# Ordering a long convolution's frequency-domain stages by two channel halves

## The chip, the cores and the metric

The kernel runs on one core of one Trainium2 chip. The metric is the device time of one execution in microseconds; smaller is better. Before the change three runs took 2891.93, 2896.40 and 2896.47 us (median 2896.4).

## The reference, cut to what matters

The program is one large block (a gated linear recurrence and a long convolution, then a mixture of 16 experts) followed by a block of two further layers. The change is inside the long convolution, for 256 positions and 1024 channels, run twice in a row (n = 0 and 1):

```python
filt = hyena_filters(S, filt_w1, filt_b1, filt_w2, filt_b2, filt_w3, filt_freq)   # taps, times a decay
z = v.astype(f32)
for n, gate in enumerate((x1, x2)):
    k = bidir_kernel(filt[:, n, 0], filt[:, n, 1])
    z = gate.astype(f32) * fftconv(z, k, filt_bias[n])     # irfft(rfft(z) * rfft(k)) + z * bias
y_b = z.astype(dt) @ w_b_out
```

Every channel is convolved by itself, so channels 0 to 511 need nothing of channels 512 to 1023 in any of these steps.

## The kernel before, in words

Five engines run programs of their own and wait for one another through semaphores. TensorE multiplies, VectorE does the two-operand arithmetic, ScalarE copies and computes functions, POOL and SP issue transfers. TensorE executes its program strictly in the written order.

The transform is done by matmuls with fixed matrices: `fwd` (two row tiles of 128 positions by 512 columns, real parts then imaginary parts of 256 frequencies) and `inv` (four row tiles by 256 positions). All data are float32. A matmul here writes 128 rows by 512 channels, one bank of `psx`. For each n the stages are, in the order of the code:

- taps (L705 to L710): 8 groups of one matmul with 64 rows of contraction, for two position tiles `tt`, two channel halves `half` and two directions `d`. VectorE (L1729 to L1744) multiplies each by the decay (into `f0` and `f1`), clears a row and adds the bias if `tt` is 0, and writes the sum and the difference into `taps_s` and `taps_d`. Below, the work for one pair of `tt` and `half` is called a quarter. When all four quarters are done it raises `taps_ready`.
- spec_k (L713 to L720): TensorE waits for `taps_ready` and transforms the taps, 8 groups of two matmuls (four row tiles `m`, two halves). ScalarE copies each group to `spec_k` in SBUF (L1294 to L1297).
- spec_u (L723 to L732): TensorE transforms the signal `v_tok`, 8 groups of two matmuls (halves, two frequency tiles `f`, real and imaginary). For n = 1 it waits for `z_tok` first. VectorE (L1745 to L1760) multiplies each by `spec_k`, reading the bank four times for one pair, and raises `spec_y` for each of the four pairs.
- inverse (L733 to L746): TensorE waits for all four steps of `spec_y`, and computes 4 groups, of 4 matmuls each for n = 0 (L739) and of 8 half-wide ones for n = 1 (L744). VectorE multiplies each by x1 (n = 0, back into `v_tok`, then `z_tok`) or by `x2` (n = 1).

The order around the change is set by a plan of banks, `small_plan()`: a list of all groups in the order in which TensorE makes them, with the engine that reads each. Four banks rotate; before a group is made, `claim` waits until the group four places earlier in the list has been read:

```python
        if g >= 4 and self.reader[g - 4]:
            pe.wait_ge(self.sems[self.reader[g - 4]], self.count[g - 4])
        return self.banks[g % 4]
```

So the order in the plan, that on TensorE and those on the readers must be the same. `was_read` waits until a group has been read, and `x_ready` until it has been made.

Behind the convolution `x2` is split into a high and a low part by ScalarE and VectorE (`cut_acts`, with the semaphore `z_cut`), and TensorE multiplies by `w_b_out` and `w_o` (L554). The weights of these products pass a ring of four buffers (SP, L2222). The experts' weights pass 16 buffers (SP, L2240); the first 16 transfers wait for `z_cut`, `merged` and the ring's last buffers, every later one for the matmuls (L813, L841) that used its buffer. POOL loads the filter's weights (the second set once the last tap group of n = 0 is made) and, behind `z_tok`, the router's weights and `memT`.

Of the kernel before, what the change touches and what calls it, by code (L numbers as in the profile page):

```python
# [25 lines left out]
TT = T // P  # L26
# [189 lines left out]
def small_plan():  # L216

    plan = []

    def add(reader, *key):  # L220
        plan.append((key, reader))

    add("act", "norm", "g_mix")
    for part in ("v", "x1"):
        for i in range(4):
            add("act", "hy_tr", part, i)
    for d in range(2):
        for kind in range(2):
            for i in range(4):
                add("act", "lru", d, kind, i)  # L230
    add("dve", "filt", 0)
    add("dve", "filt", 1)
    for n in range(2):
        for tt in range(TT):
            for half in range(2):
                for d in range(2):
                    add("dve", "taps", n, tt, half, d)
        for m in range(4):
            for half in range(2):
                add("act", "spec_k", n, m, half)  # L240
        for half in range(2):
            for f in range(2):
                for im in range(2):
                    add("dve", "spec_u", n, half, f, im)
        for i in range(4):
            add("dve", "inv", n, i)
    add("act", "norm", "g_ffn")
    add("act", "norm_mem")
    add("dve", "router")
    for tt in range(TT):  # L250
        for i in range(2):
            add("act", "h_tok", tt, i)
    for i in range(4):
        add("dve", "moe_acc", i)
    add("act", "norm", "g_final")
    for l in range(LAYERS):
        add("act", "norm", f"norm_ffn1{l}")
        for i in range(4):
            add("dve", "ffn1", l, i)
        add("act", "norm", f"norm_mix{l}")  # L260

        for i in range(3):
            add("act", "qk_norm", l, i)
        add("act", "av_tr", l, 0)
        add("act", "av_tr", l, 1)
        for h in range(6):
            for it in range(2):
                add("dve", "score", l, h, it)
        for h in range(6):
            add("act", "prob_tr", l, h)  # L270
        for q in range(HP):
            add("act", "att", l, q)
        add("act", "pool", l)

        for i in range(2):
            add("act", "kk_norm", l, i)
        for kind in range(3):
            for i in range(2):
                add("act", "lora", l, kind, i)
        if l:  # L280
            add("act", "vdown", l)
            for i in range(2):
                add("act", "vup", l, i)
        for tt in range(TT):
            for x in "abkv":
                add("dve" if x == "b" else "act", "rw_tr", l, tt, x)
            for x, r in (("A", "dve"), ("AT", "dve"), ("BT", "dve"), ("CT", "dve"), ("DT", "dve"),
                         ("P2", "act"), ("P2T", "act"), ("Q2", "dve"), ("P4", "act"), ("P4T", "act"), ("Q4", "dve"),
                         ("P8", "act"), ("Q8", "dve"), ("TR", "act"), ("X1", "act"), ("Q32", "dve"),
                         ("BV", "act"), ("WU", "act")):  # L290
                for p in range(2):
                    add(r, x, l, tt, p)
            for q in range(HP):
                add("dve", "M", l, tt, q)
                add("dve", "N", l, tt, q)
                add("dve", "RY", l, tt, q)
            for c in range(4):
                add("dve", "S", l, tt, c)
            for p in range(2):
                add("dve", "y", l, tt, p)  # L300
        for x, r in (("mean", "dve"), ("var", "act"), ("bonus", "dve")):
            for i in range(2):
                add(r, x, l, i)
        add("act", "norm", f"norm_cross{l}")
        add("act", "xnorm", l, "q", 0)
        for h in range(4):
            for it in range(2):
                add("dve", "xscore", l, h, it)
        for h in range(4):
            add("act", "xprob_tr", l, h)  # L310
        for h in range(4):
            add("dve", "xatt", l, h)
        add("act", "norm", f"norm_ffn2{l}")
        for i in range(4):
            add("dve", "ffn2", l, i)
    return plan


def program(nc, A, out):
    ctx = ExitStack()  # L320
    with ctx:
# [11 lines left out]
        def S(name):  # L333
            if name not in sems:
                sems[name] = ctx.enter_context(nc.semaphore(name))
            return sems[name]
# [197 lines left out]
        def _(pe):  # L534
# [167 lines left out]
            pe.wait_ge(S("dft_in"), 16)  # L702
            for n in range(2):
                pe.wait_ge(S(f"w3_in{n}"), 16)
                for tt in range(TT):  # L705
                    for half in range(2):
                        for d in range(2):
                            b = XB.claim(pe, ("taps", n, tt, half, d))
                            done(pe.matmul(b[:, :], sq[0:64, 2, tt * P:(tt + 1) * P], w3h[:, d, half, :],
                                           start=True, stop=True))  # L710

                pe.wait_ge(S("taps_ready"), n + 1)
                for m in range(4):  # L713
                    src = taps_s if m < 2 else taps_d
                    for half in range(2):
                        b = XB.claim(pe, ("spec_k", n, m, half))
                        for tt in range(TT):
                            mm = pe.matmul(b[:, :], fwd[:, tt, m * P:(m + 1) * P],  # L718
                                           src[:, tt, half * 512:(half + 1) * 512], start=(tt == 0), stop=(tt == 1))
                        done(mm)  # L720
                if n:
                    pe.wait_ge(S("z_tok"), 4)
                for half in range(2):  # L723
                    for f in range(2):
                        for im in range(2):
                            b = XB.claim(pe, ("spec_u", n, half, f, im))
                            m = 2 * im + f
                            for tt in range(TT):
                                mm = pe.matmul(b[:, :], fwd[:, tt, m * P:(m + 1) * P],
                                               v_tok[:, tt, half * 512:(half + 1) * 512],  # L730
                                               start=(tt == 0), stop=(tt == 1))
                            done(mm)  # L732
                pe.wait_ge(S("spec_y"), 4 * (n + 1))  # L733
                for i in range(4):
                    b = XB.claim(pe, ("inv", n, i))
                    if n == 0:
                        tt, half = i // 2, i % 2
                        for m in range(4):
                            mm = pe.matmul(b[:, :], inv[:, m, tt * P:(tt + 1) * P],  # L739
                                           spec_y[:, m, half * 512:(half + 1) * 512], start=(m == 0), stop=(m == 3))  # L740
# [392 lines left out]
        def _(act):  # L1133
# [157 lines left out]
                act.drain()  # L1291
            act.drain().then_inc(S("decay"), 1)
            for n in range(2):
                for m in range(4):  # L1294
                    for half in range(2):
                        b = x_ready(act, "spec_k", n, m, half)
                        read(copy(spec_k[:, m, half * 512:(half + 1) * 512], b[:, :]))  # L1297
            cut_acts(x2, h_hi)
            for i in range(4):
# [177 lines left out]
        def _(dve):  # L1477
# [248 lines left out]
            f0, f1 = (sq[:, i:i + 2, :].rearrange("p a t -> p (a t)") for i in (4, 6))  # L1726
            dve.wait_ge(S("bias_in"), 16)
            for n in range(2):
                for tt in range(TT):  # L1729
                    for half in range(2):  # L1730
                        cs = slice(half * 512, (half + 1) * 512)
                        for d, dst in ((0, f0), (1, f1)):
                            b = x_ready(dve, "taps", n, tt, half, d)
                            read(tt_(dst, b[:, :], decay[:, tt, cs], ALU.mult))
                        dve.drain()
                        if tt == 0:
# [4 lines left out]
                        tt_(taps_s[:, tt, cs], f0, f1, ALU.add)  # L1741
                        tt_(taps_d[:, tt, cs], f0, f1, ALU.subtract)
                        dve.drain()
                dve.drain().then_inc(S("taps_ready"), 1)  # L1744
                XB.was_read(dve, ("spec_k", n, 3, 1))  # L1745
                for half in range(2):
                    cs = slice(half * 512, (half + 1) * 512)
                    for f in range(2):
                        kr, ki = spec_k[:, f, cs], spec_k[:, 2 + f, cs]
# [11 lines left out]
                for i in range(4):  # L1761
                    b = x_ready(dve, "inv", n, i)
                    if n == 0:
                        tt, cs = i // 2, slice((i % 2) * 512, (i % 2 + 1) * 512)
                        read(tt_(v_tok[:, tt, cs], b[:, :], x1_tok[:, tt, cs], ALU.mult))
                    else:
                        read(tt_(x2[:, 2 * i:2 * i + 2, :], m2(b), x2[:, 2 * i:2 * i + 2, :], ALU.mult))
                if n == 0:
                    dve.drain().then_inc(S("z_tok"), 4)
            cut_acts(x2, "z_cut")  # L1770
            for i in range(4):
                cut_ahead(cutter, ("w_b_out", i))
# [606 lines left out]
```

## Time and profile before

| what | us |
|---|---|
| median of three runs | 2896.4 |
| profiled execution | 2899.57 |
| its span in the trace | 2897.4 |
| TensorE matmul busy | 2442.4 (84%) |
| VectorE busy | 1206.7 (42%) |
| ScalarE busy | 844.5 (29%) |

The profiled execution is one run with the recorder on; times inside it count from the start of the span. A row of the timeline gives the start, the duration, the engine, the line of the code, the operation with its output and inputs, how many such in a row, and in brackets how long the engine had been idle and what released it. One float32 matmul of the code leaves two MATMUL records. Tiles that are parts of one large tensor carry its name: `scr` and `hx` stand for nearly all the tiles of the convolution (`taps_s`, `taps_d` and `spec_y` lie in `hx`, `spec_k`, `v_tok`, `x1_tok`, `x2`, `fwd` and `inv` in `scr`), and `f0` and `f1` lie in `sq`. VectorE's two-operand operations all have the line of a helper, L1485, and ScalarE's copies L1138. The convolution runs from about 254 to 391 us.

### The profile page before, as it was taken

To read this page: it belongs to the slowest core of one execution; us is meant where nothing else is said; L and a number is where in the kernel's file an instruction comes from. 1 tells how busy PE (TensorE), PEld (TensorE's weight loads), DVE (VectorE), ACT (ScalarE), POOL (GpSimd) and SP (SyncE) were. 2 spreads that over 40 slices of the span, in tenths; PEclk is the share of its full clock that TensorE was granted. 3 is DMA by queue.
4 is the path that set the end of the run, shared out by engine and by line. 5 is a ranking of instruction groups with operands and counts; after the bars stand their busy time and mean duration, and the time that the engine had idled before them with its cause. 6 is when DMAs were issued, how large, how long until landed. Compare 5 with 4: busy or idle time off the path is not lost.

```text
span 2897.4 us, 43617 instructions
## 1 busy us (share of the span) xinstructions
PE 2442.4 (84%) x18480; PEld 1906.1 (66%) x18480; DVE 1206.7 (42%) x1767; ACT 844.5 (29%) x1204; POOL 115.5 (4%) x109
## 2 busy tenths in 40 slices
PE   6898888877777777777789997799999998779999
PEld 6896376332233332223289985689999997668999
DVE  6756453100000000000065667556556566656655
ACT  3383021100000000000044444244445444324543
POOL 0000012000000000000010010000001001000000
PEclk9998888988888888888899996789999998679999
DMA  6434036999999999999945540034555554003453
GB/s 219 152 124 153 16 132 262 425 425 425 425 424 425 425 424 425 426 425 425 426 172 187 177 168 1 30 117 141 180 189 193 179 175 139 2 30 117 162 188 117
DMA packets 118619, 669.79 MB, mean 231 GB/s; under 512 B 10683, under 2 KB 12902, under 8 KB 60993
## 3 DMA queue, kind: packets, MB, share of 16 engines
q1 hardware_dynamic: 113376, 650.14, 57.4%
q0 software_dynamic: 2784, 13.21, 1.3%
q10 hardware_dynamic: 2304, 4.20, 0.4%
q8 instruction: 120, 1.97, 0.3%
q14 instruction: 35, 0.28, 0.0%
HBM read 662.26 MB, written 5.24 MB: 230 GB/s over the span
## 4 chain that ended last, share of the span: by engine, by line
PE 52%; DMA 20%; DVE 10%; SPq 7%; ACT 3%; issue 3%; DVEq 3%; POOLq 1%; POOL 0%; ACTq 0%; PEldq 0%; PEld 0%
PE psd L554 27%; PE psx L554 8%; DMA ring<-in_w_up 7%; SPq L2240 7%; DMA ring<-in_w_down 4%; DMA hx<-in_w_down 2%; DMA ring<-in_w_gate 2%; PE psd L813 2%; DVE w_lo L1485 2%; DMA hx<-in_w_up 2%; PE psd L804 1%; PE psx L986 1%; PE psx L855 1%; PE psd L841 1%; DVE scr L1485 1%
## 5 line engine op out<-in xcount | busy, mean ns | idle before, releaser
L554 PE MATMUL psd<-h_hi,w_hi 128*128 128x256 f32 x2448 | 703.4, 287 | 51.1 <-DVEq L1515 24.9
L1485 DVE TENSOR_TENSOR w_lo<-ring,w_hi 128x1024 fp32r<-128x1024 f32 x436 | 523.4, 1242 | 450.4 <-ACT w_hi L1145 447.7
L554 PE MATMUL psd<-h_lo,w_hi 128*128 128x256 f32 x2448 | 698.0, 285 | 0.0
L554 PE MATMUL psd<-h_hi,w_lo 128*128 128x256 f32 x2448 | 697.7, 285 | 0.0
L1145 ACT ACTIVATE w_hi<-ring 128x1024 fp32r<-128x1024 f32 x436 | 435.2, 1046 | 329.6 <-PE psd L554 324.6
L554 PEld LDWEIGHTS psd<-h_hi,w_hi 128*128 128x128 f32 x2448 | 475.6, 194 | 57.1 <-DVEq L1515 26.4
L554 PEld LDWEIGHTS psd<-h_lo,w_hi 128*128 128x128 f32 x2448 | 475.7, 194 | 0.3
L554 PEld LDWEIGHTS psd<-h_hi,w_lo 128*128 128x128 f32 x2448 | 475.3, 194 | 0.0
L554 PE MATMUL psx<-halves,w_hi 128*128 128x256 f32 x1408 | 255.6, 283 | 3.2 <-issue 3.2
L554 PEld LDWEIGHTS psx<-halves,w_hi 128*128 128x128 f32 x1408 | 219.6, 192 | 3.9 <-issue 3.9
L1485 DVE TENSOR_TENSOR scr<-psd,scr 128x512 f32<-128x512 f32 x20 | 13.8, 690 | 497.8 <-PE psd L813 497.8
L554 PE MATMUL psx<-halves,w_lo 128*128 128x256 f32 x704 | 199.2, 283 | 0.0
L1138 ACT ACTIVATE scr<-psd 128x512 f32<-128x512 f32 x48 | 28.6, 596 | 579.1 <-PE psd L819 357.1
L813 PE MATMUL psd<-scr 128*32 128x512 f32 x768 | 135.0, 824 | 63.3 <-DMA scr<-in_w_up 58.1
L813 PE MATMUL psd<-ring,scr 128*32 128x512 f32 x512 | 88.2, 787 | 56.6 <-DMA ring<-in_w_up 41.5
L554 PEld LDWEIGHTS psx<-halves,w_lo 128*128 128x128 f32 x704 | 135.1, 192 | 0.0
L1842 DVE COPY scr<-psd 128x512 f32<-128x512 f32 x16 | 11.1, 692 | 294.9 <-PE psd L841 294.9
L813 PEld LDWEIGHTS psd<-scr 128*32 128x32 f32 x768 | 22.5, 129 | 164.6 <-DMA scr<-in_w_up 127.2
L554 PE MATMUL psd<-halves,w_hi 128*128 128x256 f32 x640 | 119.2, 289 | 3.0 <-DVE halves L1485 3.0
L1138 ACT ACTIVATE scr<-psx 128x192 f32<-128x192 f32 (+4 forms) x125 | 53.9, 439 | 191.9 <-PE psx L718 87.5
L554 PEld LDWEIGHTS psd<-halves,w_hi 128*128 128x128 f32 x640 | 102.4, 196 | 3.5 <-DVE halves L1485 3.2
L813 PEld LDWEIGHTS psd<-ring,scr 128*32 128x32 f32 x512 | 12.8, 121 | 121.3 <-DMA ring<-in_w_up 85.0
(344 smaller groups left out, 2942.9 us busy)
## 6 DMA issues: line engine op xcount, KB each, us to landing
ring<-in_ffn_wi SPq DMA_DIRECT2D x88, 1024.0 KB, 4.8
scr<-in_w_gate SPq DMA_DIRECT2D x48, 1024.0 KB, 19.9
scr<-in_w_down SPq DMA_DIRECT2D x48, 1024.0 KB, 22.4
scr<-in_w_up SPq DMA_DIRECT2D x48, 1024.0 KB, 27.0
ring<-in_ffn_wo SPq DMA_DIRECT2D x44, 1024.0 KB, 4.9
ring<-in_w_gate SPq DMA_DIRECT2D x32, 1024.0 KB, 19.0
ring<-in_w_up SPq DMA_DIRECT2D x32, 1024.0 KB, 26.7
ring<-in_w_down SPq DMA_DIRECT2D x32, 1024.0 KB, 22.9
```

The lines of the kernel that those rows point to most:

```text
L554: mm = pe.matmul(o, w[u], a[v], start=start and i == 0, stop=stop and i == 2, **kw)
L804: mm = pe.matmul(psd[0][:, k * CAP:(k + 1) * CAP], h_tok[:, tt, k * P:(k + 1) * P], onehot[:, tt, bass.ds(2 * pair + e, 1), :].rearrange(" ...
L813: mm = pe.matmul(psd[t // 8][32 * j:32 * j + 32, :], xs[:, t % 8, :], e_ring[s % ERING][:, j * 512:(j + 1) * 512], start=(t % 8 == 0), sto ...
L841: mm = pe.matmul(psd[2 + half][32 * j:32 * j + 32, :], actT[:, kt_ % 4, 32 * (kt_ // 4):32 * (kt_ // 4) + 32], down_rows(n)[:, j % 2, half ...
L855: pe.matmul(acc[k // 2][:, k % 2, :], ye[:, k // 4, (k % 4) * P:(k % 4 + 1) * P], PT, start=False, stop=False, skip_group_check=True)
L986: mm = pe.matmul(tri(b, n)[r, q, :], MATS[lhs][p][r, q, :], rhs(p, q)[r, :], start=True, stop=True)
L1138: return act.activation(o, i, ACT.Copy)
L1145: act.activation(w_hi[j % 2][:, c], ring[n % RING][:, c], ACT.Copy).then_inc(hi_cut, 1)
L1485: return dve.tensor_tensor(o, a, b, op)
L1842: dve.tensor_copy(ye[:, 1, :], psd[3][:, :]).then_inc(S("ye_ready"), 1)
L2240: sp.dma_start(dst, src).then_inc(e_land[s % ERING], 16)
```

## The change

Each loop over channel halves moves outside the loop over the position tiles `tt` or the row tiles `m`, in the plan and on the three engines alike. `taps_ready` is raised once for each half, and TensorE waits for it once for each half, ahead of that half's four spec_k groups. The inverse waits for two steps of `spec_y` ahead of its first two groups and for all four ahead of the last two; for n = 0 its groups are ordered so that the first two are the first half. For n = 1 they are unchanged, as group i covers channels 256 i to 256 i + 255. `z_tok` is raised in two steps of 2. No matmul and no arithmetic operation is added or taken away.

```diff
@@ small_plan
-        for tt in range(TT):
-            for half in range(2):
+        for half in range(2):
+            for tt in range(TT):
                 for d in range(2):
-                    add("dve", "taps", n, tt, half, d)
-        for m in range(4):
-            for half in range(2):
-                add("act", "spec_k", n, m, half)
+                    add("dve", "taps", n, half, tt, d)
+        for half in range(2):
+            for m in range(4):
+                add("act", "spec_k", n, half, m)
@@ TensorE
-                for tt in range(TT):
-                    for half in range(2):
+                for half in range(2):
+                    for tt in range(TT):
                         for d in range(2):
-                            b = XB.claim(pe, ("taps", n, tt, half, d))
+                            b = XB.claim(pe, ("taps", n, half, tt, d))
...
-                pe.wait_ge(S("taps_ready"), n + 1)
-                for m in range(4):
-                    src = taps_s if m < 2 else taps_d
-                    for half in range(2):
-                        b = XB.claim(pe, ("spec_k", n, m, half))
+                for half in range(2):
+                    pe.wait_ge(S("taps_ready"), 2 * n + half + 1)
+                    for m in range(4):
+                        src = taps_s if m < 2 else taps_d
+                        b = XB.claim(pe, ("spec_k", n, half, m))
...
-                if n:
-                    pe.wait_ge(S("z_tok"), 4)
                 for half in range(2):
+                    if n:
+                        pe.wait_ge(S("z_tok"), 2 * half + 2)
...
-                pe.wait_ge(S("spec_y"), 4 * (n + 1))
                 for i in range(4):
+                    if i % 2 == 0:
+                        pe.wait_ge(S("spec_y"), 4 * n + i + 2)
                     b = XB.claim(pe, ("inv", n, i))
                     if n == 0:
-                        tt, half = i // 2, i % 2
+                        tt, half = i % 2, i // 2
@@ ScalarE
-                for m in range(4):
-                    for half in range(2):
-                        b = x_ready(act, "spec_k", n, m, half)
+                for half in range(2):
+                    for m in range(4):
+                        b = x_ready(act, "spec_k", n, half, m)
@@ VectorE
-                for tt in range(TT):
-                    for half in range(2):
-                        cs = slice(half * 512, (half + 1) * 512)
+                for half in range(2):
+                    cs = slice(half * 512, (half + 1) * 512)
+                    for tt in range(TT):
...
-                dve.drain().then_inc(S("taps_ready"), 1)
-                XB.was_read(dve, ("spec_k", n, 3, 1))
+                    dve.drain().then_inc(S("taps_ready"), 1)
                 for half in range(2):
+                    XB.was_read(dve, ("spec_k", n, half, 3))
...
                     if n == 0:
-                        tt, cs = i // 2, slice((i % 2) * 512, (i % 2 + 1) * 512)
+                        tt, cs = i % 2, slice((i // 2) * 512, (i // 2 + 1) * 512)
...
-                if n == 0:
-                    dve.drain().then_inc(S("z_tok"), 4)
+                    if n == 0 and i % 2:
+                        dve.drain().then_inc(S("z_tok"), 2)
```

## Rows read from the trace of the kernel before

**Rows 1.** The page, part 4: shares of the chain that ended last, by engine.

```profile
PE 52%; DMA 20%; DVE 10%; SPq 7%; ACT 3%; issue 3%; DVEq 3%; POOLq 1%; POOL 0%; ACTq 0%; PEldq 0%; PEld 0%
```

**Rows 2.** Busy us by stretch: PE, PEld, DVE, ACT, POOL; granted clock, DMA share, GB/s.

```profile
254.00:395.00 141.00, 111.89 (x258) 53.12 (x258) 66.53 (x104) 17.63 (x26) 2.36 (x3) 0.85 0.07 23
...
460.00:510.00 50.00, 43.98 (x260) 27.95 (x263) 11.84 (x32) 6.46 (x13) 19.07 (x17) 0.79 0.57 230
510.00:1480.00 970.00, 715.90 (x4373) 314.31 (x4366) 82.12 (x142) 84.68 (x121) 5.60 (x3) 0.84 0.99 415
```

**Rows 3.** The timeline of TensorE in the convolution: start, duration, operation, count, idle before.

```profile
261.14 3.78 PE L709 MATMUL psx<-scr,sq 64*128 64x512 f32 x4 [2.66 <-DVE sq L1485]
265.12 3.78 PE L709 MATMUL psx<-scr,sq 64*128 64x512 f32 x4 [0.20 <-DVE sq L1485]
273.91 17.04 PE L718 MATMUL psx<-hx,scr 128*128 128x512 f32 x32 [5.01 <-DVEq L1744]
290.78 13.90 PE L729 MATMUL psx<-scr 128*128 128x512 f32 x32
309.14 16.49 PE L739 MATMUL psx<-hx,scr 128*128 128x512 f32 x32 [4.46 <-DVEq L1760]
325.56 5.41 PE L709 MATMUL psx<-scr,sq 64*128 64x512 f32 x12
331.72 1.98 PE L709 MATMUL psx<-scr,sq 64*128 64x512 f32 x4 [0.74 <-DVE sq L1485]
...
340.51 16.17 PE L718 MATMUL psx<-hx,scr 128*128 128x512 f32 x32 [6.81 <-DVEq L1744]
356.51 13.90 PE L729 MATMUL psx<-scr 128*128 128x512 f32 x32
374.88 15.77 PE L744 MATMUL psx<-scr,hx 128*128 128x256 f32 x64 [4.47 <-DVEq L1760]
```

**Rows 4.** The timeline of VectorE in the convolution.

```profile
264.37 1.29 DVE L1485 TENSOR_TENSOR sq<-psx,scr 128x512 f32<-128x512 f32 x2
...
268.35 1.29 DVE L1485 TENSOR_TENSOR sq<-psx,scr 128x512 f32<-128x512 f32 x2
...
271.10 1.29 DVE L1485 TENSOR_TENSOR sq<-psx,scr 128x512 f32<-128x512 f32 x2
...
292.77 1.29 DVE L1485 TENSOR_TENSOR hx<-psx,scr 128x512 f32<-128x512 f32 x2 [18.99 <-PE psx L729]
...
301.20 1.29 DVE L1485 TENSOR_TENSOR hx<-psx,scr 128x512 f32<-128x512 f32 x2
...
325.67 0.69 DVE L1485 TENSOR_TENSOR scr<-psx,scr 128x512 f32<-128x512 f32 x1 [2.74 <-PE psx L739]
...
330.97 1.29 DVE L1485 TENSOR_TENSOR sq<-psx,scr 128x512 f32<-128x512 f32 x2
```

**Rows 5.** Single microseconds by engine; the third value from the right is the granted clock.

```profile
266.00:267.00 1.00, 1.00 (x3) 0.34 (x2) 0.93 (x3) 0.00 (x0) 0.00 (x0) 0.50 0.00 0
...
281.00:282.00 1.00, 1.00 (x4) 0.48 (x3) 0.00 (x0) 0.28 (x1) 0.00 (x0) 1.00 0.00 0
...
334.00:335.00 1.00, 0.00 (x0) 0.00 (x0) 0.93 (x3) 0.00 (x0) 0.00 (x0) 0.83 0.00 0
```

**Rows 6.** The timeline of ScalarE: two of its copies of spec_k, n = 0.

```profile
282.40 0.60 ACT L1138 ACTIVATE scr<-psx 128x512 f32<-128x512 f32 x1 [1.12 <-PE psx L718]
284.12 0.60 ACT L1138 ACTIVATE scr<-psx 128x512 f32<-128x512 f32 x1 [1.12 <-PE psx L718]
```

**Rows 7.** The chain in order of time: where w_b_out starts.

```profile
394.70 25.42 PE psd L554 x192
```

**Rows 8.** The timeline of SP's transfers behind the convolution.

```profile
412.54 15.19 SPq L2240 DMA_DIRECT2D scr<-in_w_gate  x6
...
452.02 0.48 SPq L2258 DMA_DIRECT2D scr<-in_x_wkv  x1
484.91 6.51 SPq L2240 DMA_DIRECT2D scr<-in_w_down  x6
```

More of the change, by code:

```diff
@@ L1728, in _ @@
             for n in range(2):
-                for tt in range(TT):
-                    for half in range(2):
-                        cs = slice(half * 512, (half + 1) * 512)
+                for half in range(2):
+                    cs = slice(half * 512, (half + 1) * 512)
+                    for tt in range(TT):
                         for d, dst in ((0, f0), (1, f1)):
-                            b = x_ready(dve, "taps", n, tt, half, d)
+                            b = x_ready(dve, "taps", n, half, tt, d)
                             read(tt_(dst, b[:, :], decay[:, tt, cs], ALU.mult))
```

## The prediction

> **What bounds the kernel now.** First the shares of the chain of waits [rows 1]: TensorE holds about half of it, the transfers a fifth. A share over the whole span says nothing of one stage, so next the busy times by stage [rows 2]. From 510 to 1480 us the DMA engines are 0.99 busy: that is the experts' stream. The stretch that the change touches is 254 to 395 us: DMA share 0.07, ScalarE busy for 17.6 us of 141, TensorE for 111.9, VectorE for 66.5. No transfer and no third engine can set its time; it is TensorE and VectorE taking turns. Then the timeline of TensorE in it [rows 3], where the reader is to look at the idle time in brackets. It stops four times for VectorE: 5.01 us ahead of the taps' transform (L718, n = 0), 4.46 us ahead of the inverse (L739), 6.81 us ahead of L718 again (n = 1) and 4.47 us ahead of L744. The transforms of the signal (L729) have no wait ahead of them. The other side is VectorE [rows 4]: it idles for 18.99 us ahead of 292.77, while TensorE transforms the taps, and between the inverse's groups. Each stop costs twice. The granted clock [rows 5] is 1.00 in dense work, which is the 2.4 GHz level, and 0.50, which is 1.2 GHz, after a stop. ScalarE's copies [rows 6] give the price of one 512-column group of two matmuls: 1.72 us at the upper level (284.12 - 282.40). VectorE's reads of the inverse give 3.43 us for a group of four (2.74 of waiting and 0.69 of reading, at 325.67) [rows 4]. Eight groups of two, or four of four, are 13.8 and 13.7 us. The rows of the transforms are longer: 16.87 us (290.78 - 273.91), 16.42 (325.56 - 309.14), 16.00 (356.51 - 340.51) and 15.77 [rows 3]. So the lower level costs 3.1, 2.7, 2.3 and 2.0 us behind the four stops.
>
> **The change, part by part.** It removes no matmul and no vector operation. It reorders them by channel half and puts a semaphore step behind each half. The only added instructions are two more drains of VectorE for the taps and one for the product with x1.
>
> Part 1, taps to their transform, n = 0. VectorE works a quarter of the taps in 3.98 us where the row tile is 0 (268.35 - 264.37, with a memset and the bias) and 2.75 us where it is 1 (271.10 - 268.35) [rows 4]. The new order is 0, 1, 0, 1 in place of 0, 0, 1, 1, so the first half is ready 2.75 us behind 264.37, at 267.1 us. TensorE's last tap matmuls wait for the read at 264.37, which the new order has at the same time, so they start at 265.12 and end at 268.9 as now [rows 3]. The banks are claimed in written order, so the transform's first group also needs the read of the fifth tap group, at 267.1 + 0.7 = 267.8, and groups two to four need the reads at 268.5, 271.8 and 272.4. None is late. The transform starts at 268.9 instead of 273.91 and the second half's flag (273.9) is up before its first group. The whole idle time, 5.0 us, goes. The start is at the lower level: the clock is 0.50 through the taps, though TensorE is fully busy in them [rows 5]. The four starts before paid 2.0 to 3.1 us; I take 2.6, where this one paid 3.1: 0.5 more. Part 1 gives 5.5 us; bounds 5.0 and 8.1 (nothing paid for the clock).
>
> Part 2, product to inverse, n = 0. VectorE works the second half from 301.20 [rows 4] until L739 can start at 309.14 [rows 3], 4.0 us for a frequency tile, and is slower than TensorE here. So the first half's product is done at 301.1 and all of it at 309.1, both in the time of the old trace. Now inverse groups 1 and 2 need the first half alone, and the banks of spec_u's last four groups. The first of these are read by 302.5 (301.20 + 1.29) and by 303.8, one more pair of operations later, and TensorE ends L729 at 290.78 + 13.90 = 304.7 [rows 3]. So group 1 starts at 304.7, group 3 at 311.5, when the second half has been ready for 2.4 us. The stop of 4.46 us goes, and with it the 2.7 us of clock, as TensorE never halts: 7.2 us. Bounds 4.5 (the clock is lower all the same) and 7.2. VectorE's reads are behind its own product, which ends at 309.1, in both orders; four banks hold four groups, so nobody is held up.
>
> Part 3, taps to transform, n = 1. In the time of the old trace VectorE begins the second quarter at 330.97 [rows 4]; it is now a short one of 2.75, so the first half is up at 333.8. Then the bank order binds: group 1 needs a read that ends at 334.5, groups 3 and 4 the reads at 338.5 and 339.2. TensorE ends the taps at 333.7 [rows 3], starts at 334.5, does two groups to 337.9, waits 0.6 us, does two more to 341.9 and the second half's four to 348.8; the flag for that half is up at 340.6. Before it was 356.51. That is 7.7 us at the upper level. But the row of 334 to 335 us shows the clock falling within 1.3 us of the taps' end [rows 5]. If it falls here as well and two groups go at half speed, the 0.6 us wait hides a part, and the end is 350.4 to 351.1. I take 349.6, between: 6.9 us, bounds 5.4 and 7.7.
>
> Part 4, product to inverse, n = 1. As part 2: columns of groups 1 and 2 (L744) lie in the first half. 4.47 us of stop and 2.0 us of clock: 6.5 us, bounds 4.5 and 6.5. The split wait for z_tok comes to nothing: in VectorE's order all four products with x1 stand ahead of the taps of n = 1, and these ahead of all that TensorE does behind that wait.
>
> Added: three drains. A short quarter is two pairs of operations of 1.29 us and two drains, 2.75 in all, so a drain costs 0.08 us [rows 4]; only those of n = 1 lie on the path: -0.2 us, bounds 0 and -0.6. On SP and POOL nothing is moved; POOL waits for z_tok's last step and for the same last tap group as before, and its loads go out 13 us earlier, into idle DMA engines.
>
> The sum is 5.5 + 7.2 + 6.9 + 6.5 - 0.2 = 25.9 us. What follows moves along with it: cutting x2 and the first matmul of w_b_out at 394.70 [rows 7] hang on the last read; that stage starts at the lower level in the old trace and I leave it so (bound: 2.3 us more if it doesn't). The experts' first transfers [rows 8] go out at 412.54, released step by step by this chain; the last of the first sixteen has left by 452.02, and the next one leaves at 484.91, when the first expert's matmuls free a buffer. DMA share in 460 to 510 us is 0.57 [rows 2], so the stream is started by the compute chain and shifts as a whole.
>
> The profiled execution took 2899.6 us (span 2897.4 and 2.2 around it), 3.2 above the median of the runs, 2896.4. 2899.6 - 25.9 = 2873.7; on the median's footing 2870.5. All ends low: 5.0 + 4.5 + 5.4 + 4.5 - 0.6 = 18.8, so 2877.6; all high: 8.1 + 7.2 + 7.7 + 6.5 + 2.3 = 31.8, so 2864.6. The runs of before differ by 4.5 us among themselves, which widens both ends by 2 to 3 us.
>
> **The rivals.** (A) The bank rotation takes back the early start: if TensorE in truth gets no bank until the second half's last taps are read, L718 starts at 272.4 and at 339.2, and parts 1 and 3 give 1.5 and 1.3 us. Against it: the reads above, each computed from rows. Gain 16.3, time 2880. Chance 0.05.
>
> (B) Given back later: the stream or the clock of the many stages behind takes the gain, 2896. For it: those stages are two thirds of the time, and the transfers hold a fifth of the chain [rows 1]. Against: the idle DMA engines ahead of 484.91. Chance 0.04.
>
> (C) Slower: the clock. The new order lets TensorE creep along behind VectorE's reads, and the clock stays at 0.50 in all of the convolution. For it: the taps at 261 to 269 us, which stay at 0.50 for 8 us of almost unbroken work [rows 3, 5]. Against: all four transforms reach 1.00, and L729 holds it beside a slower VectorE. Price: behind 268.9 us lie six transforms of 13.8 us and the taps of n = 1 with 6.9, 89.7 us at the upper level; all at the lower they end at 448 us instead of 390.65, and the time is 2954. It decides from 52 us at the lower level more than I count on, as each costs half. Chance 0.02. The Trainium skill (TensorE: Matmul & The Clock Gate, section on psum-queue depth-cycling) speaks for it: a loop that cycles through PSUM banks and idles TensorE for short moments between groups was seen to swing between the two levels. So far the trace agrees for the taps only.
>
> **How the numbers follow.** The forecast has 0.89, A 0.05, B 0.04, C 0.02. A measurement of this kernel tells 0.2%, 5.8 us, from no change. Faster: the forecast, A, 0.94. Same: B, 0.04. Slower: C, 0.02. The range, 2862 to 2881, is the sum's bounds and the runs' spread; it takes in A.
>
> **What would show it.** In the trace after: L718 (n = 0) starts within 0.5 us of the taps' end; no idle time ahead of L739 and L744; L718 (n = 1) has two short waits of under 1 us in place of 6.81; the first w_b_out matmul stands near 369 us; granted clock 1.00 from about 274 us to the end of L739; the first refill of a buffer near 459 us. It would be wrong if L739 still waited for both halves, if the clock fell between the groups of L718, or if the first expert's matmuls didn't move by the same 26 us.

## The result and the profile after

The changed kernel took 2870.3 us (median of 4 runs, 2868.58 to 2870.71) against 2896.4 (2891.93 to 2899.29): a ratio of 0.991, 95% interval 0.9893 to 0.9927, or 26 us with 21 to 31 inside the interval. The forecast was 2870.5. The profiled execution took 2870.71 us, its span is 2868.6.

First the timeline of TensorE in the convolution of the changed kernel, to be held against [rows 3]. L718 is the taps' transform, L740 and L745 are the two inverses (L739 and L744 before).

```profile
256.69 3.70 PE L709 MATMUL psx<-scr,sq 64*128 64x512 f32 x8 [0.71 <-ACT sq L1287]
263.05 3.78 PE L709 MATMUL psx<-scr,sq 64*128 64x512 f32 x4 [2.66 <-DVE sq L1486]
267.03 3.78 PE L709 MATMUL psx<-scr,sq 64*128 64x512 f32 x4 [0.20 <-DVE sq L1486]
270.74 16.17 PE L718 MATMUL psx<-hx,scr 128*128 128x512 f32 x32
286.75 13.90 PE L729 MATMUL psx<-scr 128*128 128x512 f32 x32
300.48 13.90 PE L740 MATMUL psx<-hx,scr 128*128 128x512 f32 x32
314.31 5.41 PE L709 MATMUL psx<-scr,sq 64*128 64x512 f32 x12
320.46 1.98 PE L709 MATMUL psx<-scr,sq 64*128 64x512 f32 x4 [0.74 <-DVE sq L1486]
323.40 15.43 PE L718 MATMUL psx<-hx,scr 128*128 128x512 f32 x32 [0.95 <-DVE sq L1486]
338.67 13.90 PE L729 MATMUL psx<-scr 128*128 128x512 f32 x32
352.40 13.98 PE L745 MATMUL psx<-scr,hx 128*128 128x256 f32 x64
```

The brackets of 5.01, 4.46 and 4.47 us are gone. That of 6.81 has become 0.95, and its releaser is no longer the flag (DVEq) but a product of VectorE into `sq`, that is the read of the fifth tap group's bank. Both inverses last 13.9 to 14.0 us where they lasted 16.5 and 15.8: they run at the upper level of the clock from their first matmul.

The granted clock stands third from the right in the busy times by stretch, as in [rows 5]. It is 1.00 from 275 us to the end of the second taps, and three pieces at 0.50 are left: to 275 us, from 323 to 326 and from 371 to 374. The row of the single microsecond 322 to 323 shows that the second of these began in the idle time between the taps and L718, not among the groups of L718.

```profile
270.00:275.00 5.00, 5.00 (x6) 1.85 (x6) 4.54 (x8) 0.45 (x1) 0.51 (x1) 0.50 0.41 105
275.00:323.00 48.00, 46.70 (x108) 19.93 (x106) 25.48 (x41) 4.33 (x8) 1.85 (x2) 1.00 0.08 24
322.00:323.00 1.00, 0.45 (x2) 0.00 (x0) 0.83 (x2) 0.00 (x0) 0.00 (x0) 0.96 0.00 0
323.00:326.00 3.00, 2.60 (x3) 1.18 (x4) 2.71 (x6) 0.00 (x0) 0.00 (x0) 0.50 0.00 0
326.00:370.00 44.00, 40.38 (x126) 23.69 (x124) 23.18 (x37) 6.97 (x12) 0.00 (x0) 1.00 0.00 0
371.00:374.00 3.00, 3.00 (x16) 3.00 (x15) 0.00 (x0) 0.00 (x0) 0.00 (x0) 0.50 0.00 0
```

What follows the convolution has moved with it: the chain's first w_b_out matmul [rows 7], and SP's transfers [rows 8].

```profile
366.41 0.69 DVE scr L1486
...
370.43 24.80 PE psd L554 x192
```

```profile
387.65 15.18 SPq L2241 DMA_DIRECT2D scr<-in_w_gate  x6
...
426.95 0.44 SPq L2259 DMA_DIRECT2D scr<-in_x_wkv  x1
459.81 6.36 SPq L2241 DMA_DIRECT2D scr<-in_w_down  x6
```

To compare stages, times are counted from the first tap matmul, 254.78 us before and 256.69 after (the stage ahead of it is the same code and took 1.9 us longer in this execution).

| stretch (us) | before | after | difference |
|---|---|---|---|
| first tap matmul to first w_b_out matmul | 139.92 | 113.74 | -26.2 |
| to the first refill of an expert buffer | 90.21 | 89.38 | -0.8 |
| to the first matmul of the layers | 983.52 | 981.99 | -1.5 |
| to the end of the span | 1428.97 | 1426.80 | -2.2 |

The four differences add up to 30.7 us, and less the 1.9 us of the stage ahead they make the 28.8 us between the two spans. Only the first row is the change's. The second row varies by 2.1 us (88.07 to 90.21) among the five profiled kernels whose code behind the first w_b_out matmul is the same; 0.6 of its 0.8 us is w_b_out itself, whose row lasts 24.80 us where it lasted 25.42. The third row lies between 982.0 and 983.5 us in seven of the eight kernels profiled here (986.7 in one), the last between 1424.6 and 1429.3 us, all with the same code there, so the differences of 1.5 and 2.2 us are no effect of the change. The experts' stream took none of the gain back.

### The profile page after: what moved, and what is told of

Its sections match the earlier page's. It is cut to its first block, busy times and chain, and to the rows that moved or that the text cites. A ratio compares the mean times of both kernels' runs of the same rounds, so it can differ in the third digit from the quotient of the medians.

```text
span 2868.6 us, 43627 instructions
## 1 busy us (share of the span) xinstructions
PE 2435.4 (85%) x18480; PEld 1903.3 (66%) x18480; DVE 1206.8 (42%) x1767; ACT 844.5 (29%) x1204; POOL 115.4 (4%) x109
## 4 chain that ended last, share of the span: by engine, by line
PE 53%; DMA 21%; DVE 9%; SPq 6%; ACT 3%; issue 3%; DVEq 3%; POOLq 1%; POOL 0%; ACTq 0%; PEldq 0%; PEld 0%
PE psd L554 28%; PE psx L554 8%; DMA ring<-in_w_up 7%; SPq L2241 6%; DMA ring<-in_w_down 4%; DMA hx<-in_w_up 3%; DMA ring<-in_w_gate 2%; PE psd L814 2%; DVE w_lo L1486 2%; DMA hx<-in_w_down 2%; DMA scr<-in_w_gate 2%; PE psd L805 1%; PE psx L987 1%; PE psx L856 1%; DVE scr L1486 1%
## 5 line engine op out<-in xcount | busy, mean ns | idle before, releaser
L1843 DVE COPY scr<-psd 128x512 f32<-128x512 f32 x16 | 11.1, 692 | 287.3 <-PE psd L842 287.3
```

The source lines that it names most:

```text
L1843: dve.tensor_copy(ye[:, 1, :], psd[3][:, :]).then_inc(S("ye_ready"), 1)
```

## The experiments

Each was run beside the kernel before, in 4 or 5 timed runs. The kernel before had medians of 2896.4, 2896.7 and 2896.6 us in the three sets of runs, so the kernels of different sets are compared by their times as they stand.

**The inverse alone.** The kernel before, with the second wait split and the inverse's groups of n = 0 ordered by halves (on TensorE and VectorE), and nothing else.

```diff
-                pe.wait_ge(S("spec_y"), 4 * (n + 1))
                 for i in range(4):
+                    if i % 2 == 0:
+                        pe.wait_ge(S("spec_y"), 4 * n + i + 2)
...
-                        tt, half = i // 2, i % 2
+                        tt, half = i % 2, i // 2
```

> The kernel before with parts 2 and 4 alone: taps, their transform and both flags as before, the inverse waits for two steps of spec_y and then for all four. Theory (the four stops give their price one by one): the stops of 4.46 and 4.47 us ahead of the inverse go, with 2.7 and 2.0 us of clock; gain 13.7 us, time 2882.7, and the stops of 5.0 and 6.8 us ahead of L718 stay. Rival (only the whole order pays, since the first half is available earlier only if its taps are): gain under 5 us.

It took 2881.98 us (2879.35 to 2884.89), ratio 0.9952 (0.9938 to 0.9965). From the first tap matmul to w_b_out it is 125.9 us, 14.0 under the kernel before. The timeline of TensorE:

```profile
275.18 16.69 PE L718 MATMUL psx<-hx,scr 128*128 128x512 f32 x32 [5.01 <-DVEq L1745]
291.71 13.90 PE L729 MATMUL psx<-scr 128*128 128x512 f32 x32
305.44 13.90 PE L740 MATMUL psx<-hx,scr 128*128 128x512 f32 x32
...
334.22 16.19 PE L718 MATMUL psx<-hx,scr 128*128 128x512 f32 x32 [6.81 <-DVEq L1745]
```

The stops ahead of L718 stand to the hundredth; that ahead of the inverse is gone. The inverse needs no reordered taps. The rival is out.

**The taps alone.** The changed kernel, with one wait for all four steps ahead of the inverse.

```diff
+                pe.wait_ge(S("spec_y"), 4 * (n + 1))
                 for i in range(4):
-                    if i % 2 == 0:
-                        pe.wait_ge(S("spec_y"), 4 * n + i + 2)
```

> The changed kernel, but the inverse waits for all four steps of spec_y as before. Theory: parts 1 and 3 alone, 5.9 and 6.6 us as the trace after has them; gain 12.5 us, time 2884; a stop of 4.4 to 4.5 us stands ahead of both inverses and the clock falls behind them. With the run before this one the gains add up to 26 us. Rival (the parts overlap, one hides the other): the two gains add up to clearly more or less than 26.

It took 2884.12 us (2881.31 to 2885.48), ratio 0.9955 (0.9941 to 0.9968); the stretch is 126.8 us, 13.1 less than before. TensorE's timeline has the inverses' stops back, and not those of the taps:

```profile
286.51 13.90 PE L729 MATMUL psx<-scr 128*128 128x512 f32 x32
304.94 15.70 PE L739 MATMUL psx<-hx,scr 128*128 128x512 f32 x32 [4.53 <-DVEq L1760]
...
329.66 15.58 PE L718 MATMUL psx<-hx,scr 128*128 128x512 f32 x32 [0.95 <-DVE sq L1485]
```

The two gains in the trace are 14.0 and 13.1, together 27.1 against 26.2 for the whole change. In the medians they are 14.7 and 12.6, together 27.2 against 26.2. The parts add to within 1 us. Most of that microsecond is the clock: the inverse of n = 0 takes 15.63 us from its start to the next taps here, behind a stop of 4.53 us, and took 16.42 behind one of 4.46 in the kernel before. So what the lower level cost behind a stop of nearly one length differed by 0.8 us between these two executions.

**Keeping the clock up.** The changed kernel with matmuls of no use where TensorE idles: for n = 0 three behind the first half's taps and two behind the next pair, for n = 1 one behind the last taps, and four ahead of w_b_out. Their results are not read.

```diff
+            def fill(count):
+                for _ in range(count):
+                    pe.matmul(psd[3][:, :], fwd[:, 0, 0:P], fwd[:, 1, :], start=True, stop=True)
...
+                        if n == 0 and half + tt:
+                            if (half, tt) == (0, 1):
+                                DB.was_read(pe, ("w_a_out", 3))
+                            fill((0, 3, 2, 0)[2 * half + tt])
+                        if n == 1 and half and tt:
+                            fill(1)
...
+            fill(4)
             pe.wait_ge(S("z_cut"), 1)
```

> The changed kernel with extra float32 matmuls of 128 rows into an unused bank where TensorE idles: 3 and 2 among the taps of n = 0, 1 behind the taps of n = 1, 4 ahead of w_b_out. Their results are never read. Theory (TensorE's idle time lowers the clock, and that costs 2.25 us in L718 n = 0, 1.5 in n = 1 and 2.0 in w_b_out): granted clock 1.00 through all of it, L718 13.8 us long in both, gain over the changed kernel 5 to 6 us, time 2864.5. Rival (the taps with 64 rows of contraction pull the clock down whatever stands between them): L718 n = 0 still starts at 0.50 and the gain is 2 to 3.5 us. Second rival (a filler delays the first matmul behind it by more than the clock gives): no gain or a loss of up to 2 us.

It took 2867.88 us (2863.9 to 2869.17), 2.4 under the changed kernel in the medians and short of the 5 to 6 expected. Its convolution is 111.3 us, 2.4 less, and the first refill comes 198.06 us after the first tap matmul instead of 203.12. Of these 5.1 us, 2.4 lie in the convolution and 1.5 in w_b_out (its row lasts 23.31 us instead of 24.80, from 368.31); the other 1.2 lie between w_b_out and the refill, where kernels with the same code differ by as much, so they can't be put down to the fillers. The stretches behind the refill, the same code, were 2.1 us longer in the profiled execution. The two medians differ by less than the runs of one kernel do (2863.9 to 2869.17), so the total can't show such a part, and the stretch can. By stretch, the clock:

```profile
256.00:270.00 14.00, 12.54 (x29) 4.55 (x27) 10.12 (x16) 5.89 (x6) 0.14 (x1) 1.00 0.31 119
270.00:284.00 14.00, 13.55 (x31) 5.92 (x32) 5.59 (x10) 4.18 (x7) 0.36 (x1) 1.00 0.17 37
320.00:321.00 1.00, 1.00 (x2) 0.47 (x2) 0.83 (x3) 0.00 (x0) 0.00 (x0) 0.61 0.00 0
```

For n = 0 the first theory holds: 1.00 from the first taps through L718, and the first rival is out there. For n = 1 it fails: the clock fell at about 320.2 us, as the filler began, behind 8 us of taps with 0.74 us of idle time among them, and the gain there was nil (24.46 us from the taps to the signal's transform against 24.36). The second rival holds there: with the filler ahead of it the taps' transform starts 9.90 us behind the taps instead of 9.09, and what it then saves (14.56 us long instead of 15.27) only makes up for that. The timeline of L718 (L729 in this kernel) for n = 0 shows one thing more:

```profile
270.24 3.67 PE L729 MATMUL psx<-hx,scr 128*128 128x512 f32 x8 [0.68 <-DVE sq L1498]
274.12 10.57 PE L729 MATMUL psx<-hx,scr 128*128 128x512 f32 x24 [0.22 <-DVE sq L1498]
```

At the upper level TensorE is quick enough to meet the bank rotation: 0.68 us ahead of the first group and 0.22 ahead of the third. This is the mechanism of rival A, at 0.9 us and not at the 9.6 of its price.

**Useful matmuls in the idle time.** Behind the change TensorE is what the convolution waits for, all but while VectorE works the taps. The signal's transform doesn't depend on the taps, so the first half's four groups are put among the tap matmuls, in the four dense banks.

```diff
+                def early(g):
+                    f, im = g // 2, g % 2
+                    m = 2 * im + f
+                    if n == 0:
+                        DB.was_read(pe, ("w_a_out", g))
+                    for tt in range(TT):
+                        mm = pe.matmul(psd[g][:, :], fwd[:, tt, m * P:(m + 1) * P], v_tok[:, tt, 0:512],
+                                       start=(tt == 0), stop=(tt == 1))
+                    mm.then_inc(S("u_early"), 1)
...
+                        if (half, tt) == (0, 1):
+                            if n:
+                                pe.wait_ge(S("z_tok"), 2)
+                            early(0)
+                            early(1)
+                        elif half:
+                            early(2 + tt)
```

> The changed kernel with the first half's four spec_u groups put among the taps matmuls, into the four dense banks that are free there: two behind the first half's taps, one behind each pair of the second half's. Theory (behind the change TensorE is the bound of the convolution from the taps on, and idles only while VectorE works the taps): 6.9 us of matmuls move into idle time for n = 0 and the clock stays up, 9 us; n = 1 gains its 1.7 us of idle and 1.5 of clock; in all 12 us, time 2858. Rival (VectorE is the bound as soon as the order is loose, since a half's product takes it 8.0 us against 6.9 of TensorE): gain under 5 us, with idle time ahead of the inverse again.

It took 2858.79 us (2858.41 to 2866.69), 11.5 under the changed kernel; ratio to the kernel before 0.9868 (0.9853 to 0.9883). The timeline of TensorE for n = 0, where L719 are the taps and L711 the moved groups:

```profile
260.06 3.70 PE L711 MATMUL psd<-scr 128*128 128x512 f32 x8
263.69 1.98 PE L719 MATMUL psx<-scr,sq 64*128 64x512 f32 x4
265.60 1.98 PE L711 MATMUL psd<-scr 128*128 128x512 f32 x4
267.51 1.98 PE L719 MATMUL psx<-scr,sq 64*128 64x512 f32 x4
269.42 1.98 PE L711 MATMUL psd<-scr 128*128 128x512 f32 x4
271.24 13.90 PE L735 MATMUL psx<-hx,scr 128*128 128x512 f32 x32
284.98 7.03 PE L746 MATMUL psx<-scr 128*128 128x512 f32 x16
291.84 13.90 PE L757 MATMUL psx<-hx,scr 128*128 128x512 f32 x32
```

No bracket is left in the convolution, for n = 1 neither, and the granted clock is 1.00 in all of it (256 to 355 us); the first one stands ahead of w_b_out, 4.05 us. The stretch to w_b_out is 102.7 us, 11.1 less than in the changed kernel: 8.4 for n = 0 and 2.7 for n = 1, where 9 and 3.2 had been expected. VectorE did not become the bound. The profiled execution was the one of 2866.69 us, 8 above the three others; its excess lies behind the convolution (986.7 us of expert stream against 982.0), so only the convolution is read from it.

**The next wait for all, split too.** x2 is split into high and low parts only when all four inverse groups are multiplied, because the parts go to where `spec_y` lies, which the inverse reads to its end. Here each quarter of x2 is cut at once, into a free place (72 to 88 KiB of the scratch); in exchange two of the experts' first transfers, which go there, wait for the last w_b_out product.

```diff
+        z_halves = sb("z_halves", [P, 2 * KD * T], F32R)
...
-            pe.wait_ge(S("z_cut"), 1)
             for i in range(4):
-                dense(("w_b_out", i))
+                dense(("w_b_out", i), (z_hi, z_lo), ready=None if i else ("z_cut", 0))
@@ VectorE
+                        dve.drain().then_inc(S("act_made"), 1)
+                        low(x2, z_hi, z_lo, i, "z_cut")
@@ SP
+                elif s == ERING_SCR + 3:
+                    sp.wait_ge(slots_done, SN[("w_b_out", 3)] + 1)
```

> The changed kernel, with the split of x2 joined in the same way: each quarter of x2 is cut as soon as its inverse group has been multiplied, into a place of its own, and the first w_b_out product waits for one quarter at a time. Two of the experts' first transfers wait for the last w_b_out product in exchange. Theory (a wait for all where a part would do costs its idle time and the clock behind it): the 4.05 us ahead of w_b_out and 1.8 us of clock in it go, 5.8 us, time 2864.5. Rival (the two transfers held back, or VectorE's added steps between the inverse's reads, take it back): under 2 us of gain.

It took 2864.69 us (2861.12 to 2865.56), 5.6 under the changed kernel; ratio 0.9886 (0.9869 to 0.9903). In the trace w_b_out starts 109.3 us behind the first tap matmul, 4.4 sooner, without a stop, and its row in the chain (192 matmuls) ends 132.7 us behind it instead of 138.5: 5.8 sooner, as expected.

```profile
364.31 23.05 PE psd L557 x192
```

```profile
379.78 15.19 SPq L2244 DMA_DIRECT2D scr<-in_w_gate  x6
```

The two transfers that were held back show no cost: SP's queue reached the first six only at 379.78 us, behind the last transfers of w_o, and they took 15.19 us as in the other kernels.

**Both.** The last two together, no further edit.

> The signal's first half among the taps, as in the run with spec_u in free banks, and the split by quarters together. Theory: gains on different stops add, 11.5 + 5.8 = 17.3 us under the changed kernel, time 2853; granted clock 1.00 from the taps of n = 0 into w_o. Rival (the stages behind give a part back, as the expert stream starts from a fixed release): under 12 us.

It took 2851.36 us (2845.92 to 2852.01), 18.9 under the changed kernel and 45 under the kernel before; ratio 0.9839 (0.9824 to 0.9854). The granted clock over the whole convolution and the start of w_b_out, and w_b_out in the chain:

```profile
254.00:343.00 89.00, 88.30 (x211) 38.65 (x210) 61.39 (x97) 15.45 (x22) 2.36 (x3) 1.00 0.13 38
343.00:363.00 20.00, 20.00 (x130) 18.73 (x129) 8.04 (x12) 4.53 (x6) 0.00 (x0) 1.00 0.00 1
```

```profile
353.62 23.05 PE psd L556 x192
```

TensorE is busy for 108.3 of 109 us at 1.00. In the trace w_b_out's row ends 121.7 us behind the first tap matmul, 16.9 sooner than in the changed kernel, and that is the 11.1 and the 5.8 of the two kernels before. In the medians the single gains of 11.5 and 5.6 make 17.1, and 18.9 were measured; the difference is inside the spread of the runs (2845.92 to 2852.01). So the gains add, as expected, and the rival is out. It is the fastest version here, and with TensorE busy throughout there is next to nothing left to win in this stretch by order alone.

## Why the prediction was right

The sum was 25.9 us, the stretch gave 26.2. By the sum's own steps, read as differences of the starts of L729, the second taps, L729 again and the last read, each from the first tap matmul:

| part | forecast | measured |
|---|---|---|
| 1, taps to transform, n = 0 | 5.5 | 5.9 |
| 2, product to inverse, n = 0 | 7.2 | 7.2 |
| 3, taps to transform, n = 1 | 6.9 | 6.6 |
| 4, product to inverse, n = 1 | 6.5 | 6.4 |
| drains | -0.2 | within the parts |

The mechanism was right in all four parts. That the sum came out to 0.3 us is in part luck: parts 1 and 3 missed by 0.4 and 0.3 in opposite directions, mostly through the two prices of the clock, and one such price differed by 0.8 us between two executions above. That the median came out to 0.2 us is more luck, as the runs of one kernel differ by 2 to 11 us among themselves.

Part 1. The whole 5.01 us of idle time went, as forecast. The start at the lower level cost 2.25 us (16.01 from 270.74 to 286.75, less 13.76 for eight groups of 1.72) where I took 2.6: the clock rose after 275 us. It fell in the 2.66 us of idle time ahead of the taps at 263.05 us (0.50 from 262 us) and stayed at 0.50 through them. The run with fillers, in which both stretches hold matmuls of 128 rows, stayed at 1.00; whether it is the filled idle time or the matmuls among the taps that kept it up, that run doesn't tell.

Part 2. Exact: L740 starts right behind L729 and the clock is 1.00 throughout. The inverse-alone run shows this part by itself: 27.56 us from L729 to the second taps, in both kernels, against 34.78 before.

Part 3. The bank order bound where I said, at the fifth tap group's read: 0.95 us of idle time against 0.8. The clock did fall (0.50 from 323 us), which I had weighed and taken at half price; the row costs 15.27 us from start to start, 1.5 above the upper level. My bound for that case was worked out too kindly: two groups of 3.44 us from 334.5, then six of 1.72 end at 351.7 and not at 351.1, so the part's lower bound should have been 4.8 and not 5.4. The measured end lies at 349.9 in the time of the old trace, so this didn't bear on the outcome. The short wait ahead of the third group that I forecast isn't there, since at the lower level the first two groups took long enough to hide it. One of my signs ("two short waits") was therefore wrong, and the range of this part held it.

Part 4. As part 2.

What stayed at its price: w_b_out still starts 4.02 us behind the start of the last read, and the clock is lower behind this stop too (0.50 from 371 to 374 us, and from 393 to 399 before), as I had left it. The stream was released by the compute chain and shifted as a whole: the refill stands at 459.81 against 459 forecast, and counted from the first tap matmul it came 27.0 us sooner (203.12 for 230.13).

The rivals. A, that the bank rotation takes the early start back: its mechanism exists, at 0.95 us in the changed kernel and 0.9 in the one with fillers, not at its price. B, that a later stage gives the gain back: the stream's length is the same within 1.5 us, and in the first two experiments, too. C, the clock at 0.50 through the whole convolution: not seen in any run. The section of the Trainium skill that spoke for it (TensorE: Matmul & The Clock Gate, on psum-queue depth-cycling) describes a swing of the level when TensorE idles briefly and often between groups as it cycles through banks. The traces show single such waits only: those of 0.68 and 0.22 us ahead of and inside L718 left the clock at 1.00 in the kernel with fillers, while it fell during the one of 0.95 us behind the second taps in the changed kernel. Whether frequent ones would do what the page says, no run here shows.

## What to carry to other kernels

When two engines take turns on data whose parts are independent, look at the brackets ahead of each stage: in the kernel before each of the four stops cost its idle time and then 3 to 6 us at the lower level of the clock, and both can be read from its rows. Split such a wait only down to the first part that is ready early, check each claim of a rotating buffer against the reads behind it, and then fill what idle time is left with work that doesn't depend on it; here that was worth 11.5 us, where the change gave 26. Read small parts by stretch from a common event, as the total of this kernel wanders by 5 us.

## What the runs showed of the hardware

TensorE's idle time alone doesn't tell where the clock was up. In the changed kernel the taps, matmuls with 64 rows of contraction, ran from 263 to 270.8 us with 0.20 us of idle time between them, at 0.50 throughout; the level rose 4.3 us into L718, whose matmuls have 128 rows. With fillers the clock fell at 320.2 us behind 8 us of such taps, with under 1 us of idle time among them. In the two kernels with spec_u groups of 128 rows between the same taps it stayed at 1.00 through the convolution. That it is the rows that count, and not the short idle times between, was not tried by itself.

Nor did a stop of one length always lower the clock. In the products behind the convolution TensorE stops for 3.01 us in the changed kernel (ahead of 402.53 us) and in the last one (ahead of 383.98). In the changed kernel the granted clock was 0.50 from 402 to 408 us; in the last one it was 1.00 in the stop and in the 6 us behind it:

```profile
383.98 0.50 PE L556 MATMUL psd<-halves,w_hi 128*128 128x256 f32 x2 [3.01 <-DVE halves L1505]
```

```profile
381.00:384.00 3.00, 0.02 (x1) 0.02 (x1) 2.23 (x2) 0.63 (x1) 2.38 (x2) 1.00 1.02 431
384.00:390.00 6.00, 6.00 (x50) 6.00 (x51) 3.07 (x2) 2.01 (x2) 5.13 (x4) 1.00 0.93 340
```
